# Start addresses of SBUF tensors: multiples of 512 bytes for the large, of 64 for the small

## The chip, the cores and the metric

The kernel runs on one core of one Trainium2 chip. The metric is the time of one execution in microseconds (us) on the device. Five engines work side by side: TensorE (PE) multiplies, VectorE (DVE) and ScalarE (ACT) work on elements, GpSimd (POOL) as well, SyncE (SP) issues most transfers (DMAs). They meet through semaphores alone. SBUF, the on-chip memory, has 128 partitions; an address here is a byte within a partition, the same in all of them.

## What is computed

One decoder layer on 512 tokens of 1024 channels, in float32: a combined projection; a pooling mixer, sliding-window attention and attention into 256 memory tokens; three gated branches merged and projected; then retrieval from 16384 experts, and norms. Cut to what matters:

```python
def reference(x, mem, positions, ...):
    h = rmsnorm(x, norm1_g)
    u_pool, q, k, v, qm, gate_logits = split(h @ w_in)
    y_pool = pool_mixer(u_pool, w_pool, pool_scale)        # trailing means of 2, 4, 8, 16 tokens
    y_swa = swa_with_sinks(rope(q), rope(k), v, sinks)     # window 128
    y_mem = mem_attention(qm, rmsnorm(mem), w_mem_kv)
    g = sigmoid(gate_logits)                               # three gates
    merged = g0 * (y_pool @ w_branch_pool) + g1 * (y_swa @ w_branch_swa) + g2 * (y_mem @ w_branch_mem)
    x = x + merged @ w_out
    x = x + peer(rmsnorm(x), w_q, sub_keys, expert_u, expert_v)   # top 16 of 128 x 128 keys, 8 heads
    return rmsnorm(x, final_norm_g)
```

`peer` takes, for each token and head, the 16 best of 128 x 128 product keys and sums their experts: gate times gelu(h . u) times v.

## The kernel before

All weights come as one stream of 346 chunks (512 KB each: 128 partitions by 1024 floats). SP loads chunk n into slot n % 4 of `raw` (line 264). ACT copies it, rounded to float32r, into slot n % 2 of `w_hi` (line 761), and POOL writes the rest, raw minus w_hi, to `w_lo` (line 415). PE then forms each product in three passes of float32r: high by high, low by high, high by low. The other operand is split in the same way into a `_hi` and a `_lo` tensor. Each pass over 512 columns is one matmul. In a call `pe.matmul(bank, stationary, moving)` the second argument is loaded into the array and the third is streamed past it; the profile names a matmul "bank<-moving,stationary".

The stages, in order of time, with PE's lines:
- memory projection. Line 438 (in `product`) streams memT past w (256 columns, 4 chunks of 8 slices by 3 passes); line 492 streams w past memT (4 chunks), staying in one bank for the 3 passes of a slice.
- the projections of h for keys, values, pooling groups and queries. Line 438 streams hT past w, 24 matmuls a chunk into one bank. The attention and its softmax run between them (lines 512 to 597), to about 266 us.
- gates and branches, to about 480 us. For each of 8 column blocks, three chunks of hT (banks 0 to 2), then two chunks in which line 438 streams yT past w (banks 3 to 5).
- output projection, to about 530 us. `spread_sum` (line 635) streams w past mg. For each of 4 token tiles and 3 passes it writes the two halves of 512 columns to two banks, so the bank changes at each matmul.
- keys of the retrieval (lines 438 and 675), to about 690 us, then 128 expert chunks (hT past w, line 438) to about 1440 us. In 64 of these one-hot matmuls in bf16 (line 719, `ohI` past `ohJ`, 24 a chunk) are put between, which turn gates into rows. DVE searches the top keys beside them, then makes the one-hots.
- value stage, from about 1440 us: 128 blocks. DVE multiplies activations by gates into `wf` (line 1356), ACT makes `wT_hi` (line 992) and DVE `wT_lo` (line 1360), two slots each. PE runs `spread_sum` with w past wT, 24 matmuls a block. After that come a sum, a norm and the store, some 15 us.

SBUF is laid out by hand. An arena of 212800 bytes is allocated once; in this program it begins at byte 16512 (32 x 512 + 128). A `Place` hands out tensors one behind the other. `keep` holds x_sb, hT_hi, hT_lo, raw, w_hi, w_lo, subkeys and ident, all of sizes that are multiples of 512, then gains and the small ones. Where it ends, at `front`, the others begin, regions over each other for different stages: yT, memT, xn (`y`, `s`), then attention's (`a`) or mg, sg, part (`g`), the pooling buffers (`p`), and for the retrieval `r` (with gsm of 128 bytes ahead of I2, J2, G2, eqI, ohJ, ohI) and, behind it, `v` (a_in, g_in, wf, wT_hi, wT_lo). The offsets that result, past a multiple of 512: 128 for the eight of `keep`; 32 for yT, memT, xn, mg and all of `s`, `y`, `a`, `g` and abuf; 160 for what follows gsm, with `v`. Small sizes are rounded up to 32.

Of the kernel before, what the change touches and what calls it, by code (L numbers as in the profile page):

```python
# [18 lines left out]
T, D, P = 512, 1024, 128  # L19
# [41 lines left out]
def build(nc, dram, out):  # L61
# [4 lines left out]
    with ExitStack() as ctx:  # L66
# [3 lines left out]
        arena_at = int(nc.sbuf_base) - arena_size  # L70
        assert arena_at % 32 == 0

        class Place:
# [2 lines left out]
                self.at = at  # L76

            def __call__(self, name, shape, dt=f32):
                t = nc.alloc_sbuf_tensor_at(name, [P] + list(shape), dt, offset=arena_at + self.at)
                size = int(np.prod(shape)) * (2 if dt == bf16 else 4)  # L80
                self.at += (size + 31) // 32 * 32
                assert self.at <= arena_size, (name, self.at)
                return t

# [57 lines left out]
        sg = g("sg", [3, T])  # L142
        part = g("part", [3, T])
        p = Place(max(a.at, g.at))
        ub = p("ub", [PAD + T])
        sA = p("sA", [PAD + T])
        sB = p("sB", [PAD + T])
        rcnt = p("rcnt", [4, PAD])
        wpool = p("wpool", [4, P])
        prob1 = Place(max(a.at, g.at))("prob1", [TT, 2, 2 * WINDOW])  # L150
        assert TT * 2 * 2 * WINDOW * 4 <= p.at - max(a.at, g.at)
        prob = (prob0, prob1)
# [1304 lines left out]
```

## Time and profile before

| | before |
|---|---|
| median of 3 runs | 2159.08 us (2158.95 to 2160.14) |
| the profiled execution | 2159.83 us |
| its span, first to last instruction | 2158.0 us |
| mean granted TensorE clock | 0.992 |
| PE busy | 97% of the span |
| DVE, POOL, ACT busy | 57%, 39%, 37% |
| DMA queue 1, share of 16 engines | 44.3% |

Matmuls overlap in the profile: one is recorded for some 390 ns while the next starts after some 230. So PE's busy time tells whether PE stands still, and the distance between starts tells its pace.

### The profile page before, as it was taken

Reading aid. Unit: us, or ns where it says so; the run is one execution under the profiler, and the core shown is the slowest. Engines: PE = TensorE matmul, PEld = TensorE weight load, DVE = VectorE, ACT = ScalarE, POOL = GpSimd, SP = SyncE. Lnnn points to the kernel's source line nnn. Section 1 sums busy time; section 2 is a strip of 40 time slices with the busy share of each in tenths; the row PEclk is TensorE's granted clock in tenths of the full one; section 3 lists DMA queues with packets and bytes.
Section 4 is the critical chain, followed back from the end, with each engine's and each line's share of the span. In section 5 each row is a group of like instructions: output and inputs, shape, how many; then the busy total and the mean of one; then the engine's idle time right before and its main releaser. Section 6 shows DMA issues by size and latency. Waiting matters only on the chain.

```text
span 2158.0 us, 30302 instructions
## 1 busy us (share of the span) xinstructions
PE 2096.3 (97%) x10616; PEld 1709.1 (79%) x10616; DVE 1226.7 (57%) x1851; ACT 792.1 (37%) x1136; POOL 850.9 (39%) x361
## 2 busy tenths in 40 slices
PE   6978899999999999999999999999999999999998
PEld 5756788887888888888888888888888888888886
DVE  6688322212129999777777775025555555555555
ACT  5476422223222222344555445232222222222223
POOL 4411144443335444433333333444444444444443
PEclk9999999999999999999999999999999999999999
DMA  5211122222224444445555555675455554554552
GB/s 206 92 35 40 30 97 97 97 89 87 78 78 143 140 143 143 146 120 186 188 191 194 194 194 186 218 253 182 173 190 209 179 185 173 195 209 172 184 180 97
DMA packets 108516, 323.47 MB, mean 150 GB/s; under 512 B 11200, under 2 KB 11200, under 8 KB 106304
## 3 DMA queue, kind: packets, MB, share of 16 engines
q1 hardware_dynamic: 108192, 322.49, 44.3%
q10 hardware_dynamic: 288, 0.54, 0.1%
q8 instruction: 18, 0.29, 0.1%
q14 instruction: 18, 0.15, 0.0%
HBM read 253.78 MB, written 69.21 MB: 150 GB/s over the span
## 4 chain that ended last, share of the span: by engine, by line
PE 68%; issue 23%; POOL 9%; DVE 0%; POOLq 0%
PE bank L635 33%; PE bank L438 30%; POOL w_lo L415 9%; PE bank L719 4%; DVE x_sb L1382 0%; POOLq L414 0%; POOLq L418 0%; PE bank L703 0%; DVE x_sb L1377 0%; POOL mask L401 0%; POOL mask L399 0%; POOL mask L396 0%; POOL mask L404 0%; DVE rstd L1381 0%; POOL ident L394 0%
## 5 line engine op out<-in xcount | busy, mean ns | idle before, releaser
L415 POOL TENSOR_TENSOR w_lo<-raw,w_hi 128x1024 fp32r<-128x1024 f32 x346 | 847.2, 2449 | 1288.1 <-ACT w_hi L761 1288.1
L761 ACT ACTIVATE w_hi<-raw 128x1024 fp32r<-128x1024 f32 x346 | 366.7, 1060 | 1238.8 <-PE bank L438 700.4
L438 PE MATMUL bank<-hT_hi,w_hi 128*128 128x512 f32 x1488 | 590.9, 397 | 0.5 <-POOL w_lo L415 0.4
L438 PE MATMUL bank<-hT_hi,w_lo 128*128 128x512 f32 x1488 | 580.7, 390 | 0.0
L438 PE MATMUL bank<-hT_lo,w_hi 128*128 128x512 f32 x1488 | 579.7, 390 | 0.0
L1360 DVE TENSOR_TENSOR wT_lo<-wf,wT_hi 128x512 fp32r<-128x512 f32 x128 | 314.6, 2458 | 131.7 <-ACT wT_hi L992 131.7
L438 PEld LDWEIGHTS bank<-hT_hi,w_lo 128*128 128x128 f32 x1488 | 279.4, 188 | 59.9
L438 PEld LDWEIGHTS bank<-hT_hi,w_hi 128*128 128x128 f32 x1488 | 279.6, 188 | 59.2 <-issue 3.9
L438 PEld LDWEIGHTS bank<-hT_lo,w_hi 128*128 128x128 f32 x1488 | 279.9, 188 | 56.3 <-issue 0.7
L635 PE MATMUL bank<-w_hi,wT_hi 128*128 128x512 f32 x1024 | 321.4, 396 | 0.0
L635 PE MATMUL bank<-w_lo,wT_hi 128*128 128x512 f32 x1024 | 321.3, 396 | 0.0
L635 PE MATMUL bank<-w_hi,wT_lo 128*128 128x512 f32 x1024 | 321.3, 396 | 0.0
L1356 DVE TENSOR_TENSOR wf<-a_in,g_in 128x512 f32<-128x512 f32 x128 | 89.2, 697 | 270.7 <-PE bank L635 185.0
L635 PEld LDWEIGHTS bank<-w_hi,wT_hi 128*128 128x128 f32 x1024 | 192.4, 188 | 46.7 <-DVE wT_lo L1360 0.4
L635 PEld LDWEIGHTS bank<-w_lo,wT_hi 128*128 128x128 f32 x1024 | 192.5, 188 | 46.4
L635 PEld LDWEIGHTS bank<-w_hi,wT_lo 128*128 128x128 f32 x1024 | 192.5, 188 | 46.4
L1334 DVE TENSOR_TENSOR ohJ<-iota_b,J 128x1024 bf16<-128x1024 bf16 x64 | 164.4, 2569 | 96.5 <-PE bank L719 96.5
L983 ACT ACTIVATE gstage<-bank 128x512 f32<-128x512 f32 x128 | 129.7, 1122 | 0.0
L1337 DVE TENSOR_TENSOR ohI<-eqI,G 128x1024 bf16<-128x1024 bf16 x192 | 121.3, 686 | 9.2
L1203 DVE TENSOR_TENSOR part<-sg,bank 128x512 f32<-128x512 f32 x24 | 15.1, 683 | 175.0 <-PE bank L438 175.0
L719 PEld LDWEIGHTS bank<-ohI,ohJ 128*128 128x128 bf16 x1536 | 85.9, 98 | 16.7 <-issue 16.7
L719 PE MATMUL bank<-ohI,ohJ 128*128 128x128 bf16 x1536 | 96.8, 219 | 0.0
(217 smaller groups left out, 1519.9 us busy)
## 6 DMA issues: line engine op xcount, KB each, us to landing
raw<-stream SPq DMA_DIRECT2D x346, 512.0 KB, 3.5
a_rows<-abuf SPq DMA_DIRECT2D x128, 256.0 KB, 4.0
g_rows<-gstage SPq DMA_DIRECT2D x32, 1024.0 KB, 6.0
g_in<-g_rows SPq DMA_DIRECT2D x16, 2048.0 KB, 8.9
a_in<-a_rows SPq DMA_DIRECT2D x128, 256.0 KB, 3.5
x_sb<-x SPq DMA_DIRECT2D x4, 512.0 KB, 8.5
out<-x_sb SPq DMA_DIRECT2D x4, 512.0 KB, 2.7
subkeys<-subkeys SPq DMA_DIRECT2D x1, 1024.0 KB, 14.7
```

The lines of the kernel that those rows point to most:

```text
L415: pool.tensor_tensor(w_lo[:, k % 2, :], raw[:, k % RAW, :], w_hi[:, k % 2, :].bitcast(f32), ALU.subtract).then_inc(lo_ready, 1)
L438: last = pe.matmul(dst, w[:, slot, k * P:(k + 1) * P], rhs[low][:, r0 + k - k0, :], start=(k == k0 and wi == 0), stop=(k == k1 - 1 and wi ...
L635: last = pe.matmul(bank[2 * t + half][:, :], lhs[low_l][:, t * P:(t + 1) * P], w[:, slot, half * 512:(half + 1) * 512], start=first and lo ...
L719: last = pe.matmul(bank[2 + b][:, tk * P:(tk + 1) * P], ohJ[:, di, at, :], ohI[:, di, q, at, :], start=(q == 0), stop=(q == 2))
L761: act.activation(w_hi[:, base % 2, :], raw[:, slot, :], ACT.Copy).then_inc(hi_ready, 1)
L983: act.activation(gstage[:, half, :, t0:t0 + TOK_I // 2].rearrange("p i t -> p t i"), bank[2 + b][:, :].rearrange("p (t i) -> p t i", i=NKEYS),
L1203: dve.tensor_tensor(part[:, q, :], sg[:, q, :], bank[b][:, :], ALU.mult).then_inc(branch_read, 1)
L1334: dve.tensor_tensor(ohJ[:, di, :, :].rearrange(wide, e=2), ramp, over_keys(J2[:, toks, :]), ALU.is_equal)
L1337: last = dve.tensor_tensor(ohI[:, di, q, :, :].rearrange(wide, e=2), eqI[:, di, :, :].rearrange(wide, e=2), over_keys(G2[:, q, toks, :]), ...
L1356: dve.tensor_tensor(wf[:, di % 2, :].rearrange(tiles, b=BLOCKS), a_in[:, di % 4, :].rearrange(tiles, b=BLOCKS), g_in[:, di // GROUP, :, di ...
L1360: dve.tensor_tensor(wT_lo[:, di % 2, :], wf[:, di % 2, :], wT_hi[:, di % 2, :].bitcast(f32), ALU.subtract).then_inc(weighted_lo, 1)
```

## The change

`Place` now rounds the absolute address up, to a multiple of 512 for tensors whose size is a multiple of 512 and to a multiple of 64 for the others, where before it only rounded sizes up to 32. In the pooling region the weights `wpool` come first and the buffers behind them. Worked out for this arena: the eight tensors of `keep` go from 128 to 0, all of the regions' larger tensors from 32 or 160 to 0, ub, sA and sB to 0, 64 and 128. The highest byte in use goes from 210784 to 211776 of 212800. No instruction, semaphore or transfer is added, removed or reordered.

```diff
             def __call__(self, name, shape, dt=f32):
-                t = nc.alloc_sbuf_tensor_at(name, [P] + list(shape), dt, offset=arena_at + self.at)
                 size = int(np.prod(shape)) * (2 if dt == bf16 else 4)
-                self.at += (size + 31) // 32 * 32
+                line = 512 if size % 512 == 0 else 64
+                at = (arena_at + self.at + line - 1) // line * line
+                t = nc.alloc_sbuf_tensor_at(name, [P] + list(shape), dt, offset=at)
+                self.at = at - arena_at + size
                 assert self.at <= arena_size, (name, self.at)
                 return t
...
         p = Place(max(a.at, g.at))
+        wpool = p("wpool", [4, P])
         ub = p("ub", [PAD + T])
         sA = p("sA", [PAD + T])
         sB = p("sB", [PAD + T])
         rcnt = p("rcnt", [4, PAD])
-        wpool = p("wpool", [4, P])
```

## Rows read from the trace of the kernel before

**Rows 1.** Page: busy us, share, count of each engine; granted clock in 40 slices
```profile
PE 2096.3 (97%) x10616; PEld 1709.1 (79%) x10616; DVE 1226.7 (57%) x1851; ACT 792.1 (37%) x1136; POOL 850.9 (39%) x361
...
PEclk9999999999999999999999999999999999999999
```

**Rows 2.** Page: the chain that ended last, shares of the span by line
```profile
PE bank L635 33%; PE bank L438 30%; POOL w_lo L415 9%; PE bank L719 4%; DVE x_sb L1382 0%; POOLq L414 0%; POOLq L418 0%; PE bank L703 0%; DVE x_sb L1377 0%; POOL mask L401 0%; POOL mask L399 0%; POOL mask L396 0%; POOL mask L404 0%; DVE rstd L1381 0%; POOL ident L394 0%
```

**Rows 3.** Windows, PE: stretch, us, busy (matmuls), clock, DMA share, GB/s
```profile
700.00:880.00 180.00, 180.00 (x794) 1.00 0.48 145
...
1460.00:2140.00 680.00, 680.00 (x2916) 1.00 0.50 181
```

**Rows 4.** Timeline, PE, gates stage: start us, duration us, instruction
```profile
430.69 0.39 PE L438 MATMUL bank<-hT_lo,w_hi 128*128 128x512 f32 x1
...
441.11 0.39 PE L438 MATMUL bank<-hT_hi,w_lo 128*128 128x512 f32 x1
441.34 0.40 PE L438 MATMUL bank<-yT_hi,w_hi 128*128 128x512 f32 x1
...
449.77 0.40 PE L438 MATMUL bank<-yT_hi,w_hi 128*128 128x512 f32 x1
```

**Rows 5.** Timeline, PE, memory projection and the projection behind it
```profile
49.45 0.40 PE L492 MATMUL bank<-w_lo,memT_hi 128*128 128x512 f32 x1
...
51.78 0.39 PE L492 MATMUL bank<-w_hi,memT_lo 128*128 128x512 f32 x1
...
53.81 0.39 PE L438 MATMUL bank<-hT_lo,w_hi 128*128 128x512 f32 x1
...
59.70 0.39 PE L438 MATMUL bank<-hT_hi,w_hi 128*128 128x512 f32 x1
```

**Rows 6.** Timeline, PE, output projection
```profile
505.40 0.62 PE L635 MATMUL bank<-w_hi,mg_hi 128*128 128x512 f32 x2
...
511.00 0.62 PE L635 MATMUL bank<-w_hi,mg_hi 128*128 128x512 f32 x2
```

**Rows 7.** Groups by line: shapes, count | busy us, mean ns | idle before
```profile
L438 PE MATMUL bank<-hT_hi,w_lo 128*128 128x512 f32 x1488 | 580.7, 390 | 0.0
...
L635 PE MATMUL bank<-w_hi,wT_hi 128*128 128x512 f32 x1024 | 321.4, 396 | 0.0
...
L438 PE MATMUL bank<-yT_hi,w_hi 128*128 128x512 f32 x128 | 50.7, 396 | 0.0
...
L635 PE MATMUL bank<-w_hi,mg_hi 128*128 128x512 f32 x64 | 20.0, 393 | 0.0
```

**Rows 8.** Timeline, PE, one-hot matmuls and the next chunk's first
```profile
1004.29 1.51 PE L719 MATMUL bank<-ohI,ohJ 128*128 128x128 bf16 x24
1005.61 0.48 PE L438 MATMUL bank<-hT_hi,w_hi 128*128 128x512 f32 x1
```

**Rows 9.** Groups by line, DVE, the same operation into two tensors
```profile
L1074 DVE SCALAR_TENSOR_TENSOR hT_lo<-bank,gains,hT_hi 128x512 fp32r<-128x512 f32 x16 | 11.6, 749 | 10.0 <-ACT hT_hi L788 9.6
...
L1120 DVE SCALAR_TENSOR_TENSOR yT_lo<-bank,pscale,yT_hi 128x512 fp32r<-128x512 f32 x4 | 3.0, 746 | 1.4 <-ACT yT_hi L852 1.4
```

**Rows 10.** Timeline, engines beside PE, one block of the value stage
```profile
1701.26 2.41 POOL L415 TENSOR_TENSOR w_lo<-raw,w_hi 128x1024 fp32r<-128x1024 f32 x1 [3.19 <-ACT w_hi L761]
1701.73 2.48 DVE L1360 TENSOR_TENSOR wT_lo<-wf,wT_hi 128x512 fp32r<-128x512 f32 x1 [0.92 <-ACT wT_hi L992]
...
1705.72 1.06 ACT L761 ACTIVATE w_hi<-raw 128x1024 fp32r<-128x1024 f32 x1 [4.02 <-PE bank L635]
```

**Rows 11.** Waits of the whole span: who for whom, us in total, times, longest
```profile
ACT w_hi L761 <- PE bank L438: 700.4, 188, 6.8
ACT w_hi L761 <- PE bank L635: 530.1, 132, 4.5
...
DVE wf L1356 <- DMA a_in<-a_rows: 85.8, 4, 77.8
...
ACT memn L768 <- DMA mem_sb<-mem: 2.7, 1, 2.7
```

## The prediction

> **What bounds the kernel now.** I read the page's busy shares first: TensorE (PE) is busy 97% of the span at nearly full granted clock, every other engine (PE's own weight loads apart) under 60% [rows 1]. The chain that ended last says the same: lines 635 and 438, the two matmul loops, carry 63% of the span, and the largest piece of another engine in it is POOL's line 415 with 9% [rows 2]. PE never waits in the long stretches, so POOL's piece is a handover that came in time. The change edits no instruction, only addresses. It can therefore pay only if PE's matmuls run at a pace that depends on where their operands lie, or at the two ends, where other engines and transfers are waited for. So the next thing to read is start-to-start times. The durations of single matmuls don't serve, since they overlap: the row of line 635 says 396 ns, but one starts every 233.
>
> **Where the operands lie.** The arena begins at byte 16512 of each partition, 128 past a multiple of 512. The first eight tensors of `keep` have sizes that are multiples of 512, so hT_hi, hT_lo, w_hi, w_lo and ident all start 128 past one, which is also a multiple of 64. The small ones behind them take 928 bytes, so `front` lies 32 past a multiple of 512: yT, memT, xn and mg all start at 32. In the later region gsm's 128 bytes move what follows to 160: ohI, ohJ, wT_hi and wT_lo. Both 32 and 160 are 32 past a multiple of 64. Every slice that a float32r matmul reads starts a multiple of 512 bytes into its tensor, so it has its tensor's offset. That gives two classes of these matmuls: both operands on a multiple of 64 (hT with w), or one of them 32 off (yT or memT moving; memT, mg or wT stationary).
>
> **The pace of each class.** The windows give it for the long stretches, clock 1.00 in both: 180 us with 794 matmuls of hT and w is 226.7 ns each; 680 us with 2916 of w and wT is 233.2 ns each [rows 3]. These are different loops, so the difference could lie in the loop. The timeline gives three comparisons that hold more fixed.
> - In the gates stage one function, one line and one kind of accumulation runs first with hT, then with yT as the moving operand. From 430.69 to 441.11 lie 46 steps with hT: 226.5 ns. From 441.34 to 449.77 lie 36 steps with yT: 234.2 ns [rows 4]. The address of the moving operand is the only difference of kind.
> - Around 50 us, line 492 holds memT still and streams w, staying in a bank for at least three passes: 10 steps in 2.33 us, 233.0 ns. Just behind it, hT with w takes 26 steps in 5.89 us, 226.5 ns [rows 5].
> - The output projection streams w past mg (offset 32): 24 steps from 505.40 to 511.00, 233.3 ns [rows 6]. That is the pace of the value stage, where wT lies at 160. So 32 and 160 cost alike, which points to the distance from a multiple of 64, not of 512.
>
> I take it that a stationary operand 32 off costs about 6.6 ns, a moving one 7.7, and that both fall to 226.6 once aligned.
>
> **The change part by part.** Durations are from the profiled execution: 2158.0 us of span, 2159.83 in all, 0.75 above the median; I take the difference over to the median unchanged.
> - Value stage (line 635, wT): 3 x 1024 matmuls [rows 7], times 233.2 - 226.7 = 6.5 ns, is 20.0 us. It is on the path whole, as PE doesn't stop there. Bounds: 0 (if the stationary address is innocent) and 20.0.
> - Gates (yT): 3 x 128 [rows 7] times 7.7 ns is 2.9 us, on the path.
> - Output projection (mg): 3 x 64 [rows 7] times 233.3 - 226.5 is 1.3 us, on the path.
> - memT: 48 matmuls at line 492 (4 chunks x 2 x 2 x 3) times 6.5 ns, and 96 short ones of 256 columns at line 438 of which I count next to nothing: 0.4 us, bounds 0 and 1.
> - One-hot matmuls (line 719, bf16, both operands at 160): 24 of them take from 1004.29 to 1005.61 with the one that follows, about 56 ns each [rows 8]. 128 columns at the granted 2.4 GHz are 53.3 ns (1.00 is that level), so 1536 of them can return 0 to 4.4 us. I take 0: what they lose above their columns is 2.7 ns, while even an aligned float32r matmul loses 13. Below nothing is possible by the rival of the slow side only.
> - The projections with hT (3 x 1488 = 4464 matmuls [rows 7]) and everything else that reads `keep` move from 128 to 0. Offsets 32 and 160 behave alike, so I take 0.
> - Vector and scalar work: DVE's form of three operands takes 749 ns into hT_lo (offset 128) and 746 into yT_lo (offset 32) [rows 9]. I cost the alignment of DVE and ACT at nothing. POOL's subtractions have all operands at 128 already. A DVE or ACT that was a little faster or slower would be covered anyway: see the next point. If that cover were gone, 128 subtractions of 2.48 us each would stand in the open.
> - What is late next in the value stage: for one block w_lo is there at 1701.26 + 2.41 = 1703.67 and wT_lo at 1701.73 + 2.48 = 1704.21; the next block's start frees ACT at 1705.72 [rows 10]. PE begins a block each 5.60 us and would begin one each 5.44. The late one has 1.5 us in hand and keeps 1.35.
> - Transfers: ACT's wait ahead of w_hi ends with PE, 700 and 530 us, not with a load; the one place where a load of the start is seen is 2.7 us on mem_sb, and wf's wait for a_in is a single long one before the stage [rows 11]. A row that starts on 512 bytes can move the first load by some tenths either way: 0, bounds -0.5 and +0.5. The DMA engines are half idle. In the attention stage small plain matmuls lie 32 off too; I take 0, with bounds of -1.5 and +1.5 chosen for its mix of short waits. New addresses let new buffers share bytes (wpool now lies under prob1's first part instead of its last), but no wait is added and no queue is passed.
>
> The sum: 20.0 + 2.9 + 1.3 + 0.4 = 24.6 us. 2159.1 - 24.6 = 2134.5 us.
>
> **Two rules of the Trainium skill against it.** Within one stage yT costs 234.2 ns and hT 226.5 [rows 4]. The Trainium skill, "SBUF — State Buffer", section on the DMA port swizzle, describes lines of 16 bytes with a penalty for each crossing. A start at 32 lies on such a line, so by that rule nothing changes and the time stays 2159.1; the trace disagrees, and the rule is rival B. The best pace in the rows is 226.5 ns for 512 columns [rows 4]. The Trainium skill, "TensorE: Matmul & The Clock Gate", section "Wait — 56ns, not 53.3ns?", gives columns over 2.4 GHz plus about 2.5 ns when warm, 215.8 here, with no word on alignment; the bf16 rows agree (56), the float32r rows don't. If 512-byte starts were what it takes, rival C would follow; by that page it would give 88 us on top, an estimate.
>
> **The rivals.**
> - A: the moving operand's address matters, the stationary's doesn't, and line 635 is slow for its form: it changes the bank at each matmul and uses w as moving operand. For it: no row shows that form aligned. Against it: line 492 has the w form without changing banks at each step and runs at 233.0. Then only yT's 2.9 us and 0.1 of memT go: 2156.1 us.
> - B: addresses don't matter, the classes differ by something else (the region of SBUF, say), or the start offsets on the chip aren't those of the program, so that the change doesn't do what it says: 2159.1 us.
> - C: the remaining 226.6 - 213.3 = 13.3 ns of all 8112 float32r matmuls of 512 columns (4464 + 384 + 192 + 3072) also hang on the start, and multiples of 512 remove up to all of it: as low as 2134.5 - 108 = 2027 us. Against it: 32 and 160 don't differ.
> - D, slower: what makes hT's class fast is the start at 128, not at a multiple of 64, and starts at 0 (all operands in step) are as slow as at 32. The place is line 438: 4464 hT matmuls times 6.7 ns is +29.9 us, with the value stage left as it is: 2189 us. It decides from 24.6 us over 4464, 5.5 ns per hT matmul, if the other classes gain all the same. Against it: w and hT stand exactly in step now and are the fastest pair. For it: no row has a start at 0.
>
> **How the numbers follow.** The forecast 0.80, A 0.08, B 0.05, C 0.03, D 0.04. The forecast's own range: down by the one-hot matmuls' 4.4, attention's 1.5, start's and memT's 1.1 and some 3 of a base that falls a little, to 2124; up by the same small terms and by a third of the value stage's gain not coming, to 2143. It holds the 0.80, so it is the range. What a measurement of this kernel can tell from no change is about 0.2%, 4.3 us; A and B fall within it. Faster 0.83, same 0.13, slower 0.04.
>
> **What would show it.** Right: in the value stage a start each 226 to 227 ns (2916 matmuls in about 661 us), yT in the gates at hT's pace, hT's own pace unchanged, line 719 near 56 ns, ACT's and DVE's durations unchanged. A: yT at 227 and wT still at 233. C: hT below 226. D: hT at 233. Wrong in another way: PE showing waits on wT_lo or w_lo in the value stage, which the slack of 1.35 us excludes, or a granted clock below the 1.00 of this window [rows 3].

## The result and the profile after

| | before | after |
|---|---|---|
| median | 2159.01 us (2158.59 to 2160.14, 4 runs) | 2133.94 us (2132.51 to 2135.68, 4 runs) |
| the profiled execution, its span | 2159.83, 2158.0 us | 2133.81, 2132.0 us |
| mean granted clock | 0.992 | 0.991 |

The ratio is 0.9883, with a 95% interval of 0.9871 to 0.9894: 25.1 us less, 1.2%. The engines' part of the page, and its chain of work that ended last:

```profile
PE 2071.6 (97%) x10616; PEld 1708.8 (80%) x10616; DVE 1226.4 (58%) x1851; ACT 792.1 (37%) x1136; POOL 849.2 (40%) x361
...
PE bank L637 32%; POOL w_lo L417 19%; DMA a_in<-a_rows 0%; POOLq L416 0%; DVE x_sb L1384 0%; DMA a_rows<-abuf 0%; POOLq L420 0%; DVE x_sb L1379 0%; DVE wf L1358 0%; POOL mask L401 0%; POOL mask L403 0%; SPq L266 0%; DVE wT_lo L1362 0%; ACT wT_hi L994 0%; POOL mask L398 0%
```

PE's busy time is down by 24.7 us, that of the others by at most 1.7. Line numbers are two higher now. The chain draws POOL's handovers with 19% where it had 9%; in the whole span PE waits 0.4 us for w_lo, once, so this is how the chain was followed and no new bound. The windows of PE (stretch, us, busy with matmuls, clock, DMA share, GB/s):

```profile
700.00:880.00 180.00, 180.00 (x794) 1.00 0.49 144
1460.00:2110.00 650.00, 650.00 (x2870) 1.00 0.52 188
```

hT with w runs as before, 794 matmuls in 180 us [rows 3]. The value stage has 2870 in 650 us, 226.5 ns each against 233.2. The timeline of the gates, where one chunk pair of yT lies between two of hT, and of the output projection:

```profile
437.58 0.39 PE L440 MATMUL bank<-yT_hi,w_hi 128*128 128x512 f32 x1
...
448.46 0.39 PE L440 MATMUL bank<-hT_hi,w_hi 128*128 128x512 f32 x1
```

```profile
497.42 0.61 PE L637 MATMUL bank<-w_hi,mg_hi 128*128 128x512 f32 x2
...
508.30 0.61 PE L637 MATMUL bank<-w_hi,mg_hi 128*128 128x512 f32 x2
```

Both stretches are 48 matmuls in 10.88 us, 226.7 ns, where yT had 234.2 [rows 4] and mg 233.3 [rows 6]. So the four classes that carry the time, with hT, yT, mg and wT, have the one pace now. The fifth, w past memT (48 matmuls early in the kernel, in short stretches between waits), comes from 233.3 to 229.4 ns on the mean of its steps without a wait: after a gap some five of its steps still take 228 to 236 ns before the pace settles at 227. In the value stage the other engines come as early as before (groups as in [rows 10]):

```profile
1704.40 2.40 POOL L417 TENSOR_TENSOR w_lo<-raw,w_hi 128x1024 fp32r<-128x1024 f32 x1 [3.04 <-ACT w_hi L763]
1704.87 2.48 DVE L1362 TENSOR_TENSOR wT_lo<-wf,wT_hi 128x512 fp32r<-128x512 f32 x1 [0.92 <-ACT wT_hi L994]
...
1708.70 1.06 ACT L763 ACTIVATE w_hi<-raw 128x1024 fp32r<-128x1024 f32 x1 [3.86 <-PE bank L637]
```

wT_lo is there at 1707.35, the next block starts at 1708.7: 1.35 us in hand. By stage, from the first matmul of each kind to that of the next, the value stage to its last matmul (us, profiled executions):

| stretch | before | after | gain |
|---|---|---|---|
| first matmul to first hT | 43.30 | 44.73 | -1.4 |
| to first yT (projections, attention, first gates) | 222.90 | 220.32 | 2.6 |
| to first mg (gates) | 204.48 | 201.28 | 3.2 |
| to the transposes behind it | 47.31 | 46.01 | 1.3 |
| to the first one-hot matmul | 380.20 | 380.74 | -0.5 |
| to the value stage | 523.20 | 522.76 | 0.4 |
| value stage | 716.79 | 696.52 | 20.3 |

The first two rows don't follow any layout: in the runs below the second lies between 220.1 and 224.1, and the kernel with yT alone off has 222.7, where everything that runs there has the same offset past a multiple of 512 as in the changed kernel. I read nothing into them.

### The profile page after: what moved, and what is told of

The parts are those of the page before. It is cut to its first block, busy times and chain, and to the rows that moved or that the text cites. A ratio compares the mean times of both kernels' runs of the same rounds, so it can differ in the third digit from the quotient of the medians.

```text
span 2132.0 us, 30302 instructions
## 1 busy us (share of the span) xinstructions
PE 2071.6 (97%) x10616; PEld 1708.8 (80%) x10616; DVE 1226.4 (58%) x1851; ACT 792.1 (37%) x1136; POOL 849.2 (40%) x361
## 4 chain that ended last, share of the span: by engine, by line
issue 47%; PE 32%; POOL 19%; DMA 1%; POOLq 0%; DVE 0%; SPq 0%; ACT 0%
PE bank L637 32%; POOL w_lo L417 19%; DMA a_in<-a_rows 0%; POOLq L416 0%; DVE x_sb L1384 0%; DMA a_rows<-abuf 0%; POOLq L420 0%; DVE x_sb L1379 0%; DVE wf L1358 0%; POOL mask L401 0%; POOL mask L403 0%; SPq L266 0%; DVE wT_lo L1362 0%; ACT wT_hi L994 0%; POOL mask L398 0%
## 5 line engine op out<-in xcount | busy, mean ns | idle before, releaser
L417 POOL TENSOR_TENSOR w_lo<-raw,w_hi 128x1024 fp32r<-128x1024 f32 x346 | 845.5, 2444 | 1264.1 <-ACT w_hi L763 1264.1
L637 PE MATMUL bank<-w_hi,wT_hi 128*128 128x512 f32 x1024 | 315.3, 389 | 0.1
L637 PE MATMUL bank<-w_lo,wT_hi 128*128 128x512 f32 x1024 | 315.3, 389 | 0.0
L637 PE MATMUL bank<-w_hi,wT_lo 128*128 128x512 f32 x1024 | 315.2, 389 | 0.0
```

Of the source, the lines that this page charges most:

```text
L417: pool.tensor_tensor(w_lo[:, k % 2, :], raw[:, k % RAW, :], w_hi[:, k % 2, :].bitcast(f32), ALU.subtract).then_inc(lo_ready, 1)
L637: last = pe.matmul(bank[2 * t + half][:, :], lhs[low_l][:, t * P:(t + 1) * P], w[:, slot, half * 512:(half + 1) * 512], start=first and lo ...
```

## The experiments

The prediction held one theory of the cause, that a start off a multiple of 64 costs time. The changed kernel can't test it: it puts everything on multiples of 512 at once. All kernels below but two are the changed kernel with some tensors put elsewhere, through an offset added to `Place`:

```diff
-            def __init__(self, at):
-                self.at = at
+            def __init__(self, at, off=0):
+                self.at, self.off = at, off
...
-                at = (arena_at + self.at + line - 1) // line * line
+                at = (arena_at + self.at - self.off + line - 1) // line * line + self.off
```

"At 32" means 32 past a multiple of 512. Times are medians on the device, or a single run where no range is given; those kernels are read by the pace in their traces, and their time is only compared with the sum of it; the kernel before stood at 2160.2 to 2160.6 beside them.

**Value stage alone.**

```diff
+        v.off = 32
         wT_hi = v("wT_hi", [2, T], f32r)
         wT_lo = v("wT_lo", [2, T], f32r)
+        v.off = 0
```

> The changed kernel with wT_hi and wT_lo alone put 32 past a multiple of 512; everything else stays on its multiple. My theory (a float32r matmul is slow when either operand starts off a multiple of 64): line of spread_sum with wT at 233.2 ns a start, the value stage 20 us longer, 2134 + 20 = 2154 us. Rival (the value stage gained from something else that moved: wf, a_in, g_in, or w going from 128 to 0): 226.7 ns and 2134 us. All other stages unchanged under both.

Measured 2154.0 us (2152.38 to 2154.45). PE's window:

```profile
1460.00:2100.00 640.00, 640.00 (x2745) 1.00 0.51 186
```

That is 233.2 ns; the value stage takes 716.80 us, as before the change, and the other classes stay at 226.7. The address of the loaded operand is the cause of 20 of the 25 us, and rival A of the prediction, which holds it innocent, falls.

**yT alone** (`y = Place(front, 32)`).

> The changed kernel with yT_hi and yT_lo alone at 32. Theory: yT's matmuls at 234 ns in place of 226.7, 384 of them, +2.9 us, 2137 us; hT's in the same stage stay at 226.7. Rival (region or stage, not the start): 226.7 for both and 2134 us.

Measured 2137.22 us (2135.0 to 2137.59). 48 matmuls of yT take 11.20 us, 233.3 ns:

```profile
441.32 0.40 PE L440 MATMUL bank<-yT_hi,w_hi 128*128 128x512 f32 x1
...
452.52 0.40 PE L440 MATMUL bank<-hT_hi,w_hi 128*128 128x512 f32 x1
```

The gates take 204.1 us against 201.3. The streamed operand counts too.

**Multiples of 64 without multiples of 512.** The kernel before, with one line changed:

```diff
-                self.at += (size + 31) // 32 * 32
+                self.at += (size + 63) // 64 * 64
```

> The layout of before, with sizes rounded up to 64 in place of 32 and nothing else: keep's large tensors stay 128 past a multiple of 512, the regions lie on multiples of 64 that are no multiples of 512, wpool stays behind its buffers. Theory (64 is the step that counts, 512 and the order of wpool do nothing): 226.7 ns in every float32r class and 2134 us, like the changed kernel. Rival (512 counts): between 2134 and 2159, with wT and yT above 226.7.

Measured 2138.08 us (2136.45 to 2138.74), which looks like a near miss. The trace shows that it isn't one. wT runs at 226.7 ns (first fence), but yT and mg, both now at 0, are as slow as ever: 11.19 us for 48 of yT, 11.21 for 48 of mg.

```profile
1460.00:2100.00 640.00, 640.00 (x2825) 1.00 0.53 191
```

```profile
439.16 0.40 PE L438 MATMUL bank<-yT_hi,w_hi 128*128 128x512 f32 x1
...
450.35 0.39 PE L438 MATMUL bank<-hT_hi,w_hi 128*128 128x512 f32 x1
...
500.27 0.63 PE L635 MATMUL bank<-w_hi,mg_hi 128*128 128x512 f32 x2
...
511.48 0.63 PE L635 MATMUL bank<-w_hi,mg_hi 128*128 128x512 f32 x2
```

In this layout w lies at 128, yT and mg at 0, wT at 128. All are multiples of 64. Fast are those that lie where w lies, hT and wT.

**keep at 32, the regions at 0** (`keep = Place(0, 32)`, and `keep.off = 0` behind ident).

> The changed kernel with the large tensors of keep (x_sb, hT, raw, w, subkeys, ident) all at 32 and the regions at 0. Now hT and w stand in step with each other, both 32 off. Theory (each operand off costs its own price: moving 7.7, stationary 6.6 ns): hT with w at about 241 ns, that is +14 ns on 4464, +64 us; the value stage with moving w 32 off at about 234, +22 us; yT, mg and memT stages +3; together about 2223 us. Variant (one price however many are off): hT with w at 234, +32 us, together about 2191 us. Rival (operands have to be in step, not on a multiple of 64): hT with w at 226.7, only the value stage and yT's slower, about 2159 us. POOL's subtraction, now with three operands 32 off, stays at 2.44 us if only PE cares.

Measured 2158.49 us (2157.25 to 2159.74): the number of the rival with "in step". PE's windows:

```profile
700.00:880.00 180.00, 180.00 (x795) 1.00 0.49 145
1460.00:2100.00 640.00, 640.00 (x2744) 1.00 0.51 186
```

hT with w, both at 32, keep 226.4 ns, though neither lies on a multiple of 64. The value stage, with w at 32 and wT at 0, is at 233.2. My theory of a price for each operand off its multiple is dead. What counts is how the two starts lie to each other: operands that start the same number of bytes past such a multiple are in step. POOL, with all three operands at 32, takes 2441 ns for a subtraction against 2444 with them at 0.

**Which distances.** Two kernels with other places for yT, mg and wT; w and hT stay at 0. Starts that are no multiples of 32 are made as slices of a longer tensor.

```diff
+        def shifted(place, name, shape, off):
+            size = int(np.prod(shape))
+            t = place(name, [2 * size + 128], f32r)
+            return [t[:, off // 4 + i * size:off // 4 + (i + 1) * size].rearrange("p (a b) -> p a b", a=shape[0])
+                    for i in range(2)]
...
+        y.off = 256
...
+        g.off = 64
...
+        wT_hi, wT_lo = shifted(v, "wT", [2, T], 16)
```

> The changed kernel (w and hT at 0) with yT at 256, mg at 64 and wT at 16. New theory: what counts is the distance between the starts of the streamed and the loaded operand modulo 512; 0 is fast (226.7 ns), every other costs 6.6 (233.3), at whatever distance: yT, mg and wT all at 233, together 2134 + 2.8 + 1.3 + 20 = 2158 us. Rival 1 (modulo 256): yT at 226.7. Rival 2 (modulo 32 or coarser steps only, so 16 is as good as 0): wT at 226.7 and 2138 us. Rival 3: the price grows with the distance: wT cheapest, yT dearest.

Measured 2153.11 us. mg at 233.3 and wT at 233.1 ns, but yT, at 256, at 226.7 (10.88 us for 48):

```profile
437.09 0.39 PE L451 MATMUL bank<-yT_hi,w_hi 128*128 128x512 f32 x1
...
447.97 0.39 PE L451 MATMUL bank<-hT_hi,w_hi 128*128 128x512 f32 x1
```

The second has yT at 16, mg at 256, wT at 384.

> The same with yT at 16, mg at 256 and wT at 384. New theory (any distance modulo 512 but 0): all three classes at 233, 2158 us. Modulo 256: mg at 226.7, the others at 233. A step of 32: yT at 226.7.

Measured 2152.9 us. mg, at 256, at 226.7 (10.88 us for 48), yT at 231.6, wT at 232.4 ns. At a distance of 256 both yT and mg have the pace of 0, at 384 wT hasn't: the modulus is 256, and in step means a multiple of 256 bytes apart. And a distance of 16 is not as good as 0.

```profile
500.03 0.62 PE L648 MATMUL bank<-w_hi,mg_hi 128*128 128x512 f32 x2
...
510.91 0.62 PE L648 MATMUL bank<-w_hi,mg_hi 128*128 128x512 f32 x2
```

**Only the low halves off** (yT_lo, mg_lo, wT_lo at 32, the high ones at 0).

> The changed kernel with only the low halves yT_lo, mg_lo and wT_lo at 32. A third of each class is out of step: a third of the price, 6.8 + 0.9 + 0.4 = 8 us, 2142 us. In the value stage the six matmuls of a tile are two with w_hi and wT_hi, two with w_lo and wT_hi, two with w_hi and wT_lo. If the price belongs to a matmul's own pair, the two last are slow (starts after them late). If it belongs to a stream and the load that runs beside it, which is that of the next matmul, the fourth and the fifth are slow. The rest at 226.7.

Measured 2154.21 us, a miss of 12 us, 9 of them in the value stage. A third of the pairs is out of step and three quarters of the price is paid: the value stage takes 712.3 us (696.5 in step, 716.8 out of it), 231.9 ns a matmul. Neither version of "whose price" held. In a tile of six the median distances are 233, 231, 233, 235, 231, 231 ns; none of the six is at 227, not even the two with w_hi and wT_hi in step. The longest is the fourth: its own operands are in step, and the next load, which is wT_lo's, is the first that isn't. The timeline shows twelve in 2.78 us:

```profile
1700.38 0.63 PE L646 MATMUL bank<-w_lo,wT_hi 128*128 128x512 f32 x2
...
1702.71 0.62 PE L646 MATMUL bank<-w_hi,wT_hi 128*128 128x512 f32 x2
1703.16 0.63 PE L646 MATMUL bank<-w_lo,wT_hi 128*128 128x512 f32 x2
```

**w at 128, all else at 0.** Every start is a multiple of 128.

```diff
+        keep.off = 128
         w_hi = keep("w_hi", [2, D], f32r)
         w_lo = keep("w_lo", [2, D], f32r)
+        keep.off = 0
```

> The changed kernel with w_hi and w_lo alone at 128; all else at 0, so every start is a multiple of 64 and of 128. New theory (distance modulo 512): all 8112 float32r matmuls of 512 columns are out of step and cost 6.6 ns more: 53.5 us, 2134 + 53.5 = 2188 us, slower than the kernel before by 29. My old theory (multiples of 64): 226.7 ns everywhere and 2134 us. Distances modulo 128: 2134 us too.

Measured 2173.44 us (2166.09 to 2174.59), ratio to before 1.0049 (1.003 to 1.0068): slower than before. The direction is that of the new theory, the size is short of it. The windows:

```profile
700.00:880.00 180.00, 179.89 (x772) 1.00 0.48 140
1460.00:2100.00 640.00, 640.00 (x2755) 1.00 0.53 190
```

hT comes to 233.2 ns by the window with its few gaps, 232.7 start to start, and wT to 232.3: the price at this distance is 5.7 to 5.9 ns for hT, yT and wT and not 6.6, which only mg pays (233.3). Of the 40 us over the changed kernel's span, 17.4 are in the value stage, 7.8 before the one-hots, 6.5 among them, 5.1 in the gates, 2.1 behind the one-hots, 1.3 with mg. Attention and its projections show 1.1, within their scatter, and the stretch ahead of them is 1.4 shorter.

**w at 256, all else at 0** (the same diff with 256).

> The changed kernel with w_hi and w_lo alone at 256, all else at 0. From the two single classes measured at a distance of 256 (226.7 and 226.8 ns): all float32r classes at 226.7, 2134 us, like the changed kernel. Rival (there it was yT or mg that stood at 256, not w; a layout in which the weights do could still lose): hT with w above 230 and up to 2174 us, as with w at 128.

Measured 2133.78 us (2132.47 to 2135.16), ratio 0.9881 (0.9864 to 0.9897), all classes at 226.7 ns. From w at 128 to w at 256 are 39.7 us.

```profile
700.00:880.00 180.00, 180.00 (x795) 1.00 0.49 144
1460.00:2100.00 640.00, 640.00 (x2826) 1.00 0.53 191
```

**Blocks in step and out of step in turn, and the one-hot matmuls.**

```diff
+        r.off = 32
         ohJ = r("ohJ", [2, TOK_I, NKEYS], bf16)
+        r.off = 0
...
+        def slots(name):
+            t = v(name, [2 * T + 128], f32r)
+            return t[:, 0:2 * (T + 8)].rearrange("p (a b) -> p a b", a=2)[:, :, 0:T]
```

> The changed kernel with slot 0 of wT_hi and wT_lo at 0 and slot 1 at 32, so that blocks of 24 matmuls in step and out of step alternate in the value stage; and ohJ, the loaded operand of the bf16 one-hot matmuls, at 32 with ohI at 0. Theory (an out-of-step matmul throws the sequence out of a settled order, which comes back within some ten matmuls, as behind yT in the kernel before): blocks of slot 1 at 233, blocks of slot 0 slow for up to ten matmuls and then at 226.7, so some 12 to 14 of the 20 us come back: about 2147 us. Rival (the price is each pair's own): half of it, 2144 us, with every matmul of slot 0 at 226.7. Rival 2 (never settles while disturbed): all at 232 to 233, 2154. The bf16 matmuls: 56.3 ns as now if only float32r, which reads 4 bytes a column, pays; up to 59 if every kind does, 4 us more.

Measured 2144.59 us: half the price, close to what the rival "each pair's own" has. A block in step and the one behind it, out of step:

```profile
1702.36 0.62 PE L643 MATMUL bank<-w_lo,wT_hi 128*128 128x512 f32 x2
...
1707.35 0.62 PE L643 MATMUL bank<-w_hi,wT_hi 128*128 128x512 f32 x2
1707.81 0.63 PE L643 MATMUL bank<-w_lo,wT_hi 128*128 128x512 f32 x2
...
1712.95 0.62 PE L643 MATMUL bank<-w_hi,wT_hi 128*128 128x512 f32 x2
```

22 matmuls in 4.99 us are 226.8 ns, 22 in 5.14 are 233.6. The pace changes within two matmuls of the block's edge; here nothing takes ten to settle. But the edge isn't where the pair's own operands change. The step that follows the last matmul of a block in step, whose own two operands are in step, takes 235 ns in all 64 blocks, where the one before it takes 226 or 227. In the trace the load for the next matmul, the first out of step, begins beside that matmul's stream:

```profile
1707.12 0.42 PEld L643 LDWEIGHTS bank<-w_hi,wT_hi 128*128 128x128 f32 x2
```

On the way back the last step out of step takes 232 or 233 ns, though the load beside it is in step again, and the next one 231 in most blocks; the third is at 227. So the slow pace sets in with the first load out of step and outlasts the last by two steps. Elsewhere it outlasts it longer: in the gates of the kernel before, hT's first nine steps behind each yT pair take 2.08 us, 231 ns each, though hT and w are in step.

```profile
424.98 0.39 PE L438 MATMUL bank<-hT_hi,w_hi 128*128 128x512 f32 x1
...
427.06 0.39 PE L438 MATMUL bank<-hT_hi,w_hi 128*128 128x512 f32 x1
```

The one-hot matmuls stay at 56.3 ns, the mean by the starts in the trace, with their operands 32 apart (24 between 1005.78 and 1007.11 here, [rows 8] there):

```profile
1005.78 1.51 PE L727 MATMUL bank<-ohI,ohJ 128*128 128x128 bf16 x24
1007.11 0.48 PE L446 MATMUL bank<-hT_hi,w_hi 128*128 128x512 f32 x1
```

So bf16 matmuls of 128 columns don't pay at this distance. Whether that is the type or the short stream, no run separates.

**More distances:** yT at 192, mg at 224, wT at 4.

> The changed kernel with yT at 192, mg at 224 and wT at 4. Theory (any distance that is no multiple of 256 costs 5 to 7 ns): all three classes at 232 to 234, about 2158 us. Rival (a short distance of less than 16 bytes is free): wT at 226.7 and 2138 us.

Measured 2155.14 us: yT and mg at 233.3, wT at 232.4 ns. Even 4 bytes, one element, cost nearly the whole price.

```profile
1460.00:2100.00 640.00, 640.00 (x2755) 1.00 0.53 187
```

**The kernel before with two gaps.** If the distance is all, this must do what the change did:

```diff
-        front = keep.at
+        front = keep.at + 96
...
         gsm = r("gsm", [TT * PEER_H])
+        r.at += 128
```

> The kernel before, not the changed one, with 96 bytes left free ahead of the regions and 128 behind gsm; nothing else. keep's large tensors stay at 128, yT, memT and mg come to 128, wT and what lies behind gsm to 384: every streamed operand of a float32r matmul lies a multiple of 256 from its loaded one, though nothing large begins on a multiple of 512 or even 256. If the distance modulo 256 is all that the change bought: 226.7 ns in every class and 2134 us. If the multiples of 512 themselves, the small tensors or wpool's place do part of it: above that, up to 2159 us.

Measured 2132.56 us (2132.25 to 2134.37), ratio 0.9874 (0.9858 to 0.989): the changed kernel's time within their spreads.

```profile
700.00:880.00 180.00, 180.00 (x794) 1.00 0.48 144
1460.00:2100.00 640.00, 640.00 (x2825) 1.00 0.53 191
```

224 bytes of gaps in the old layout bring the whole gain. The multiples of 512, the small tensors on 64 and wpool's place bring nothing that these runs can see.

**Matmuls of 256 columns.** The same traces hold one more class of float32r matmul, memT streamed past w with 256 columns (line 438 before, 440 after), and for it the rule turns round. The last stretch of it, before (distance 160) and after (distance 0):

```profile
25.41 0.28 PE L438 MATMUL bank<-memT_hi,w_lo 128*128 128x256 f32 x1
...
27.90 0.28 PE L438 MATMUL bank<-memT_hi,w_lo 128*128 128x256 f32 x1
```

```profile
26.03 0.28 PE L440 MATMUL bank<-memT_hi,w_lo 128*128 128x256 f32 x1
...
28.55 0.28 PE L440 MATMUL bank<-memT_hi,w_lo 128*128 128x256 f32 x1
```

21 steps take 2.49 us out of step, 118.6 ns each, and 2.52 us in step, 120.0. In all kernels the same 21 steps are at 119.4 to 120.0 ns in the ten that have memT in step, and at 118.3 to 118.7 in the four that haven't (before, sizes to 64, keep at 32, w at 128). Being out of step makes this class 1.3 ns quicker, not slower. With 96 such matmuls that is 0.1 us here, but the price belongs to matmuls of 512 columns and can't be carried over to shorter ones.

All classes of 512 columns but w past memT together; distance is the streamed operand's start minus the loaded one's, modulo 256. The pace is that of the windows, or of 48 matmuls in the timeline, or the mean of the starts in the trace without the gaps:

| distance | class and kernel | ns |
|---|---|---|
| 0 | hT in all kernels but w at 128; yT, mg, wT after; yT or mg 256 away; w 256 away | 226.4 to 226.8 |
| 252 | wT at 4 | 232.4 |
| 16, 240 | yT at 16; wT at 16 | 231.6; 233.1 |
| 32 | yT at 32; w at 32 with wT, mg at 0; mg at 224 | 233.3; 233.3; 233.3 |
| 96, 160 | before: mg; yT | 233.3; 234.2 |
| 128 | w at 128: hT, yT, wT, mg; wT at 384; sizes to 64: yT, mg | 232.7, 232.4, 232.3, 233.3; 232.4; 233.1, 233.5 |
| 192 | yT at 192; mg at 64 | 233.3; 233.3 |
| 224 | before: wT; wT at 32; keep at 32: yT | 233.2; 233.2; 233.4 |

## Why the prediction was right, and where it wasn't

The time was forecast at 2134.5 us and came at 2133.94. The terms, by the stage table, where the profiled executions differ by 26.0 us: the value stage 20.0, came 20.3. The gates 2.9, came 3.2; hT's first matmuls behind each yT pair, slowed before as well, are the rest (nine steps of hT there take 2.08 us, as shown above, where nine at 226.7 take 2.04; there are seven such places). The output projection 1.3, came 1.3. These three are 24.8 of the 26.0; the other 1.2 are the sum of four stretches between -1.4 and 2.6 that follow no layout. The one-hots 0, came 0 (56.3 ns before and after; [rows 8] read as one block give 55.0 and not "about 56", as the step from the last one-hot to hT is 29 ns). hT at its old pace; DVE's pair of operations at 749 and 747 ns [rows 9]; the hand that wT_lo keeps 1.35 us, as worked out. memT was forecast at 0.4 and gives 0.1 at most: its 48 matmuls of 512 columns gain 3.9 ns on the mean and not 6.5, 0.2 us, and its 96 of 256 columns lose 0.1. Rivals A, B, C and D fell by the result (A: wT comes to 226.7; D: hT would be at 233; C: hT stays at 226.7, so multiples of 512 take nothing from what is left above 213.3; the 215.8 of the Trainium skill, "TensorE: Matmul & The Clock Gate", section "Wait — 56ns, not 53.3ns?", isn't reached by the pace of any float32r class here).

The time came as forecast, but a step of the reasoning failed, the sentence "32 and 160 cost alike, which points to the distance from a multiple of 64, not of 512". The starts were compared with a grid, and should have been compared with each other. w lay at 128, so mg was 96 away, wT 32 away and yT 96 away on the other side, and only hT was 0 away. The rows could not separate "on a multiple of 64" from "where the other one lies", since the only pair of the first kind was also the only pair of the second. I had seen the second: rival D's "against" says that w and hT "stand exactly in step now and are the fastest pair". But I used it as a counter to D instead of making it a rival. It would have given the same 2134.5 us for this change, since a layout with every large tensor at 0 satisfies both rules. That the number came out is luck in this point. So the number was right and its reason half right: the time does hang on addresses, stage by stage as costed, but through the distance of the two operands modulo 256. The difference is not academic: the layout that keeps every start on a multiple of 128 and breaks the step costs 39.5 us (w at 128, 2173.4), and the theory in the prediction gives it 2134.

The two prices of the prediction, 7.7 ns for a moving and 6.6 for a stationary operand, were no matter of the role either: yT, moving, costs 6.6 at 32 (233.3), and the 7.7 belong to its distance of 160.

Two sizes failed after that. The price isn't the same at each distance, and not even at one: yT at a distance of 128 takes 233.1 ns with the sizes rounded to 64 and 232.4 with w at 128. With w at 128 it is 5.7 to 5.9 ns for all but mg, which makes 6 of the 15 us by which this kernel came under the 2188 expected. Most of the rest is price that doesn't reach the span, by the number of hT's matmuls at 5.9 ns against the stages' lengths: 2.4 us among the one-hots, 1.9 ahead of the first yT, 1.4 in the stage of the keys. The start was 1.4 us shorter besides. And a third of the pairs out of step (low halves) cost three quarters of the price and not a third.

On the page that spoke against the change: by the Trainium skill, "SBUF — State Buffer", section on the DMA port swizzle, starts at 32 would cost nothing, since they lie on its lines of 16 bytes. The runs disagree, and more plainly than the rows of before did: 16 bytes, a whole such line, cost 4.9 and 6.4 ns (yT and wT).

What stays open is the mechanism. The trace shows the load for the next matmul begin beside the stream of the one before it (1707.12 in the kernel with blocks), and the slow pace sets in with the first such load that is out of step. A collision of the two reads, 2048 bytes a partition streamed and 512 loaded, in a memory that repeats every 256 bytes would fit that and the modulus. It is not shown: no kernel changed when a load runs against a stream. It doesn't explain why matmuls of 256 columns lose nothing, nor why the slow pace outlasts what is out of step by two steps in one place and by nine in another. The low-halves kernel would fit a pace that is disturbed again before it has recovered, but no run tests that.

## What to carry to other kernels

Where TensorE bounds a kernel in float32r, read the distance between starts of successive matmuls by operand pair; a few ns that differ between pairs of the same shape point to addresses. Let all operands that meet in a matmul of 512 columns start the same number of bytes past a multiple of 256: here 3% of a matmul, 1.2% of the kernel, for 224 bytes of gaps. For shorter streams measure first: those of 256 columns were 1% quicker the other way. A layout in which one small tensor shifts all that follow loses it silently, and an explanation found by comparing offsets has to be tried with a layout in which the explanations part.

## What the runs showed of the hardware

- A float32r matmul of 128 x 128 by 512 columns, back to back at the granted clock 1.00 in long stretches of one kind, starts every 226.7 ns when its streamed and its loaded operand start a multiple of 256 bytes apart, and every 231.6 to 234.2 ns at each of the nine other distances seen (4 bytes off to 128). In step they were seen both at 0, both at 32, both at 128, 256 apart, and at 128 and 384, all at this pace.
- With 256 columns it is 119.4 to 120.0 ns in step and 118.3 to 118.7 at distances of 32, 128 and 160.
- In step, 512 columns take 13.4 ns and 256 columns 13.3 ns more than one column a cycle at 2.4 GHz would (213.3 and 106.7 ns): as far as two sizes tell, an amount per matmul and not per column.
- bf16 matmuls of 128 columns, ohI past ohJ: 56.3 ns at distances 0 and 32.
- POOL's subtraction of 1024 elements: 2441 ns with operands at 32, 2444 at 0. DVE's three-operand form: 746 to 749 ns at either.
- In the value stage, blocks of 24: the slow pace sets in one step ahead of the first matmul out of step (235 ns in 64 of 64 blocks) and ends two steps behind the last load out of step. Behind yT in the gates of the kernel before, it takes hT nine steps, 231 ns each. With pairs of both kinds mixed in sixes, all become slow.
